# An encoder layer with a mixture of experts: the order of merge, output projection and top-k for two groups of tokens

## Chip, cores, metric

One core of a Trainium2 chip. The metric is the device time of the kernel in microseconds: the median of the runs shown.

## The reference, cut to what matters

One layer is applied to two groups that share all weights: a prompt of 256 tokens (2 tiles of 128) and a sample of 1024 (8 tiles), model width 1024.

```python
h = rms_norm(x) * (1 + sc1) + sh1
[qA|kA|vA|qB|kB|vB|gA|gB] = h @ w_in
oa = global_attention(...) @ w_branch_a          # 8 heads, all keys of the group
ob = window_attention(...) @ w_branch_b          # 8 heads, |i - j| <= 128, "banded"
x  = x + gt1 * ((sigmoid(ga) * oa + sigmoid(gb) * ob) @ w_out)
h2 = rms_norm(x) * (1 + sc2) + sh2
aff = softmax(h2 @ w_router)                     # 16 experts
g, idx = top_k(aff.T, cap)                       # per group; cap 128 (sample), 32 (prompt)
ye = (silu(h2[idx] @ w_gate[e]) * (h2[idx] @ w_up[e])) @ w_down[e] * g
y = rms_norm(x + gt2 * scatter_add(ye, idx))
```

The top-k of a group needs the affinities of all its tokens, and the first expert needs the indices of both groups.

## The kernel before

**Split products.** The projections from the merge on, and the experts, are done as three bf16 products (`split_product`): each operand is cut into a bf16 high half and the rest, low half. So each operand needs a high-half copy and a subtraction first. `HS` does it for the normed input h on POOL, `NM` for attention outputs on POOL, `WS` for a block of merge weights (ScalarE high, VectorE low), `WO` for w_out, POOL inside `M` for the merged activations.

**The plan.** `plan_steps` returns one list of steps. Every engine walks the same list and does its own part of each step, in that order; semaphores tie the parts together. So a step that stands early in the list holds all later ones of the same engine. SyncE has a program of its own that issues the loads in a fixed order, each behind a wait.

**The stages, in order.** Attention items (`S`, `MX`, `EX`, `T`, `PV`); the last 40 items are banded, four to a group, and `HS` of all ten tiles is placed at every second of them. Then the merge: for each m of eight 128-column blocks of the output, `("M", m, c)` computes gA, gB and the two branch projections for 512, 512 and 256 tokens (c = 0, 1, 2; prompt and sample in one row of 1280 tokens). A block's weights (1.5 MB: six DMAs in `mw_load`, rows of 512 bytes) land in one staging area `mw` and are split into one of two buffers `mws`; the next load waits for that split (`ws_done`). Then the projection: `("O", t)` for ten tiles, prompt first; `XO` adds the residual and normalizes, `X2` transposes and modulates, `RT` is router and softmax, `AT` transposes affinities into `affP` or `affS`. `GT` 0 to 3 broadcast gate 1, `GT` 4 to 7 gate 2. `("K", 0)`, the prompt's top-k, stands after the seventh tile; after the last tile come `GT` 4 to 7, `("K", 1)`, the sample's top-k, and `I`, which transposes indices and weights. In `topk` (L1059) a round takes the largest 8 with three scans of the list (L1062 to L1064): 16 rounds over 1024 affinities for the sample, 4 over 256 for the prompt, 16 experts on 16 partitions.

**Experts.** Weights come in chunks of 2 MB: `load_chunk`, three staging areas (`stage`: gate, up, down), split by halves into six slots (ScalarE L803 high, VectorE L1302 low). The first eight halves (`AHEAD`) are prepared before expert 0: ScalarE's high halves in step `("K", 1)`, the low halves by POOL (L751). SyncE sends chunks 0 and 1 of expert 0 after the last output tile (L595) and each further one when a staging area is free. Expert 0's rows are gathered by two indirect DMAs on POOL (L700), transposed, modulated by VectorE (L1294) and split by POOL (L713, L716). Expert 0 has sixteen groups of gate and up products, four to a quarter; later experts also carry the down products of the one before.

## Time and profile before

| | us |
|---|---|
| median of 3 runs | 2573.92 |
| lowest, highest | 2571.49, 2574.54 |
| the profiled execution, its time | 2572.49 |
| its span, first to last instruction | 2570.7 |
| TensorE busy in it | 2384.8 (93%) |
| VectorE busy | 1605.4 (62%) |
| ScalarE busy | 1162.8 (45%) |
| POOL busy | 1123.0 (44%) |
| mean granted TensorE clock | 0.964 of full speed |

The page cuts the span into 40 slices of 64 us and gives the busy share of each engine in tenths. TensorE is at 8 or 9 everywhere but in slices 18 and 19 (1093 to 1221 us) and the last. Busy shares don't say what a stage waits for; the waits, the chain of work that ended last and the timelines do. Engines are named PE (TensorE), DVE (VectorE), ACT (ScalarE), POOL and SP (SyncE) in the rows; `arena` is the one large SBUF buffer that holds nearly all tiles.

### The profile page before, as it was taken

What the parts mean: (1) busy time and instruction counts of PE and PEld (TensorE: products, weight loads), DVE (VectorE), ACT (ScalarE), POOL (GpSimd) and SP (SyncE); (2) the same over time, 40 slices, a digit from 0 to 9 for tenths busy, and PEclk for the clock granted to TensorE, in tenths of its full rate; (3) what the DMA queues carried; (4) which work ended last, traced back from release to release, by engine and by line L of the source; (5) the groups of instructions that cost most, each with busy time, mean ns of one, the idle gap of its engine ahead of it and who ended that gap; (6) DMA issues with size and microseconds to landing.
All of it is one profiled execution on the core that took longest, in us unless ns stands there. A gap on an engine that the chain in (4) does not pass through costs nothing.

```text
span 2570.7 us, 53875 instructions
## 1 busy us (share of the span) xinstructions
PE 2384.8 (93%) x23508; PEld 1712.8 (67%) x23508; DVE 1605.4 (62%) x2014; ACT 1162.8 (45%) x1468; POOL 1123.0 (44%) x721
## 2 busy tenths in 40 slices
PE   8999899998999999934899999999999999999993
PEld 3444477655555555523788888888888888888871
DVE  1643466556111125575888878887888878887862
ACT  2111455567111112330656655665556655556552
POOL 0000111146232331042657667776677666676640
PEclk9999899999999999956999999999999999999997
DMA  8100300220221103252889998999899998999965
GB/s 315 33 17 1 115 1 1 99 99 2 82 50 50 25 34 115 99 207 76 300 317 330 324 318 321 326 336 320 312 331 318 343 315 317 331 330 326 315 234 188
DMA packets 230113, 512.23 MB, mean 199 GB/s; under 512 B 7819, under 2 KB 35580, under 8 KB 229756
## 3 DMA queue, kind: packets, MB, share of 16 engines
q1 hardware_dynamic: 219324, 477.36, 52.3%
q0 software_dynamic: 10560, 31.46, 4.4%
q8 instruction: 186, 3.05, 0.5%
q14 instruction: 43, 0.35, 0.0%
HBM read 480.49 MB, written 28.31 MB: 198 GB/s over the span
## 4 chain that ended last, share of the span: by engine, by line
PE 85%; DVE 6%; POOL 2%; SPq 2%; ACT 1%; DMA 1%; issue 1%; DVEq 0%; POOLq 0%; ACTq 0%
PE ps L1403 21%; PE ps L1404 20%; PE ps L1405 20%; PE ps L1472 7%; PE ps L1688 4%; PE ps L1533 3%; PE ps L1545 3%; PE ps L1514 2%; DVE arena L1054 1%; DVE ti_s L1063 1%; DVE top_s L1062 1%; DVE arena L1064 1%; POOL arena L679 1%; PE ps L1625 1%; POOL arena L676 1%
## 5 line engine op out<-in xcount | busy, mean ns | idle before, releaser
L1403 PE MATMUL ps<-arena 128*128 128x160 bf16 (+2 forms) x5344 | 1308.6, 264 | 21.8 <-DVE arena L1335 8.3
L1404 PE MATMUL ps<-arena 128*128 128x160 bf16 (+2 forms) x5344 | 1308.6, 264 | 0.0
L1405 PE MATMUL ps<-arena 128*128 128x160 bf16 (+2 forms) x5344 | 1308.4, 264 | 0.0
L1302 DVE TENSOR_TENSOR arena<-arena 128x2048 bf16<-128x2048 f32 x376 | 919.2, 2450 | 193.3 <-ACT arena L803 192.3
L803 ACT ACTIVATE arena<-arena 128x2048 bf16<-128x2048 f32 x384 | 726.7, 1904 | 239.0 <-PE ps L1405 176.9
L1403 PEld LDWEIGHTS ps<-arena 128*128 128x128 bf16 x5344 | 524.1, 98 | 154.6 <-issue 27.0
L1405 PEld LDWEIGHTS ps<-arena 128*128 128x128 bf16 x5344 | 524.3, 98 | 127.8 <-issue 1.9
L1404 PEld LDWEIGHTS ps<-arena 128*128 128x128 bf16 x5344 | 524.3, 98 | 118.9 <-issue 1.4
L727 POOL TENSOR_TENSOR arena<-arena 128x320 bf16<-128x320 f32 x128 | 283.8, 2217 | 10.0
L724 POOL TENSOR_TENSOR arena<-arena,ones 128x320 bf16<-128x320 f32 x128 | 179.4, 1401 | 179.3 <-DVE arena L1335 179.0
L991 ACT ACTIVATE arena<-ps 128x160 f32<-128x160 f32 x256 | 77.4, 303 | 351.4 <-PE ps L1405 351.4
L1472 PE MATMUL ps<-arena 128*128 128x512 f32 x480 | 208.1, 593 | 3.0 <-DMA arena<-w_in 1.7
L656 POOL TENSOR_TENSOR arena<-ones,rinv 128x512 f32<-128x512 f32 x20 | 20.9, 1043 | 393.9 <-DVE rinv L1206 337.0
L1240 DVE TENSOR_TENSOR arena<-arena,ps 128x512 f32<-128x512 f32 (+1 forms) x48 | 26.6, 595 | 246.5 <-ACT arena L956 246.5
L1472 PEld LDWEIGHTS ps<-arena 128*128 128x128 f32 x480 | 90.3, 190 | 113.8 <-issue 109.5
L956 ACT ACTIVATE arena<-ps 128x512 f32<-128x512 f32 (+1 forms) x48 | 22.6, 523 | 263.5 <-PE ps L1405 263.5
L686 POOL TENSOR_TENSOR arena<-arena 128x512 f32<-128x512 f32 (+1 forms) x24 | 26.1, 1088 | 217.9 <-DVE arena L1240 217.9
L713 POOL TENSOR_TENSOR arena<-arena,ones 128x480 bf16<-128x480 f32 (+1 forms) x48 | 101.4, 2113 | 45.4 <-DVE arena L1294 45.4
L911 ACT ACTIVATE arena<-ps 128x512 f32<-128x512 f32 (+2 forms) x160 | 74.5, 494 | 102.4 <-PE ps L1533 97.8
L1533 PEld LDWEIGHTS ps<-ident,arena 128*128 128x128 f32 x752 | 81.7, 143 | 55.0 <-issue 44.7
L1054 DVE TENSOR_SCALAR arena<-ps,A,modT 128x128 f32<-128x128 f32 x160 | 52.8, 402 | 97.9 <-PE ps L1458 97.9
L1335 DVE TENSOR_TENSOR arena<-arena,ps 128x160 f32<-128x160 f32 x256 | 79.2, 310 | 55.3 <-POOL arena L727 38.4
(197 smaller groups left out, 2377.8 us busy)
## 6 DMA issues: line engine op xcount, KB each, us to landing
arena<-w_e_gate SPq DMA_DIRECT2D x64, 2048.0 KB, 9.1
arena<-w_e_up SPq DMA_DIRECT2D x64, 2048.0 KB, 9.5
arena<-w_e_down SPq DMA_DIRECT2D x64, 2048.0 KB, 9.2
arena<-w_ada SPq DMA_DIRECT2D x12, 2048.0 KB, 8.6
arena<-x_sample SPq DMA_DIRECT2D x16, 512.0 KB, 3.5
arena<-w_in SPq DMA_DIRECT2D x16, 512.0 KB, 5.3
arena<-w_in SPq DMA_DIRECT2D x3, 2048.0 KB, 21.0
arena<-w_out SPq DMA_DIRECT2D x2, 2048.0 KB, 8.0
```

Source lines behind the costliest of these rows:

```text
L713: gp.tensor_tensor(xeT[par][:, 0, d0:d1], src, ones[:, 0:d1 - d0].unsqueeze(2).to_broadcast([P, d1 - d0, SLOTS]), ALU.mult).then_inc(high, 1)
L724: gp.tensor_tensor(hidT[par][:, 0, f:f + 2], src, ones[:, 0:2].unsqueeze(2).to_broadcast([P, 2, SLOTS]), ALU.mult).then_inc(high, 1)
L727: gp.tensor_tensor(hidT[par][:, 1, f:f + 2], src, hidT[par][:, 0, f:f + 2], ALU.subtract).then_inc(hid_done, 1)
L803: ac.activation(split_half(slot, a)[0], stage_half(kind, a), ACT.Copy).then_inc(hi_done, 1)
L1302: ve.tensor_tensor(lo, stage_half(kind, a), hi, ALU.subtract).then_inc(lo_done, 1)
L1335: ve.tensor_tensor(hid32[:, f % 4], sil[:, f % 2], ps[:, f % 3, SLOTS:2 * SLOTS], ALU.mult)\
L1403: pe.matmul(out, w_hi, x_hi, start=start, stop=False)
L1404: pe.matmul(out, w_hi, x_lo, start=False, stop=False)
L1405: return pe.matmul(out, w_lo, x_hi, start=False, stop=stop)
L1472: ins = pe.matmul(ps[:, n % 5], hT[:, kk, t * P:(t + 1) * P], wqkv[c][:, kk, :], start=(kk == 0), stop=(kk == KD - 1))
L1533: ins = pe.transpose(b[:, q * P:(q + 1) * P], probs(i, hh)[:, (a + q) * P:(a + q + 1) * P], ident[:])
L1688: ins = pe.matmul(ps[32 * g:32 * g + 32, 5, 0:256], x, wv[n][:, kf, 256 * g:256 * g + 256], start=q + kf == 0 and x is x_hi and n == 0, st ...
```

## The change

- The merge runs for the sample alone first: `("M", m, 0)` and `("M", m, 1)`, 512 tokens each. The splits of w_out (`WO`) stand before the last of these parts instead of after it.
- Then the output projection of the eight sample tiles (`O` 0 to 7). Tiles are now numbered by position p, and `tile_at(p)` puts the prompt's tiles last (positions 8 and 9).
- Then the merge for the prompt, `("M2", m, b)`: b = 0, 1 are its two halves, 256 tokens, the same products as the old c = 2. Its eight weight blocks are loaded a second time into the same `mw`, and split into `mws2`: the high half by ScalarE, of the low half 1024 elements by VectorE (`ws_done`) and 2048 by POOL (`ws_rest`). The first two loads and splits are placed among the output tiles; load 2 stands behind all residual loads in SyncE's order, and each next one behind both parts of the split before it. Loads of expert chunks 0 and 1 follow loads 3 and 4.
- The sample's top-k is cut into two half lists of 512 on partitions 0 to 15 and 32 to 47, 16 rounds (`KR`) for both at once, placed between the blocks of `M2` (0, 0, 2, 3, 3, 3, 3, 2 rounds). `KM` merges the two sorted halves in ten small operations. `GT` 4 to 7 are placed inside blocks 3 and 4.
- Then `O` 8 and 9; the last inner step of `O` 8 waits for block 7's merged part. After them the prompt's top-k and `I`.
- `HS` stands at every third banded item, for the sample's eight tiles; the prompt's two come after the attention. q and o are laid out tile by tile.
- The low halves of the first eight expert weight halves are done by VectorE: four before expert 0's rows are modulated and four after.

```diff
+def tile_at(p):
+    return (p + PT_TILES) % NT
...
             c += 1
-        if i >= first_b + 11 and i % 2 and hs < NT:
+        if i >= first_b + 11 and (i - first_b) % 3 == 2 and hs < NT - PT_TILES:
             s.append(("HS", hs))
             hs += 1
         if i == len(items):
             s += [("A2",), ("WS", 0)]
-    assert hs == NT
+    assert hs == NT - PT_TILES
+    s += [("HS", p) for p in range(hs, NT)]
     assert t == len(items) and pv == len(items) and len(normed) == len(items) // NPAIR and s_ac == 12
     for m in range(KD):
         s.append(("M", m, 0))
         if m + 1 < KD:
             s.append(("WS", m + 1))
-        s.append(("M", m, 1))
         if m == KD - 1:
             s += [("WO", 0), ("WO", 1)]
-        s.append(("M", m, 2))
-    for t in range(NT + 3):
-        if t < NT:
-            s.append(("O", t))
-        if t == 0:
+        s.append(("M", m, 1))
+    ns = NT - PT_TILES
+    for p in range(ns):
+        s.append(("O", p))
+        if p == 0:
             s += [("GT", n) for n in range(4)]
-        if 0 <= t - 1 < NT:
-            s.append(("X2", t - 1))
-        if 0 <= t - 2 < NT:
-            s.append(("RT", t - 2))
-        if 0 <= t - 3 < NT:
-            s.append(("AT", t - 3))
-        if t == 6:
-            s.append(("K", 0))
-        if t < NT:
-            s.append(("XO", t))
-    s += [("GT", n) for n in range(4, 8)]
-    s += [("K", 1), ("I",)]
+        if p >= 1:
+            s.append(("X2", p - 1))
+        if p >= 2:
+            s.append(("RT", p - 2))
+        if p >= 3:
+            s.append(("AT", p - 3))
+        s.append(("XO", p))
+        if p in (1, 3):
+            s.append(("WS", KD + p // 2))
+    tail = {(0, 1): [("X2", ns - 1), ("RT", ns - 2), ("AT", ns - 3)], (1, 0): [("RT", ns - 1), ("AT", ns - 2)],
+            (1, 1): [("AT", ns - 1)], (3, 0): [("GT", 4)], (3, 1): [("GT", 5)], (4, 0): [("GT", 6)], (4, 1): [("GT", 7)]}
+    r = 0
+    for m in range(KD):
+        for b in range(2):
+            s.append(("M2", m, b))
+            s += tail.get((m, b), [])
+        if m + 2 < KD:
+            s.append(("WS", KD + m + 2))
+        for _ in range((0, 0, 2, 3, 3, 3, 3, 2)[m]):
+            s.append(("KR", r))
+            r += 1
+    assert r == CAP_S // 8
+    s += [("O", ns), ("KM",), ("XO", ns), ("O", ns + 1), ("X2", ns), ("XO", ns + 1), ("RT", ns), ("AT", ns), ("X2", ns + 1),
+          ("RT", ns + 1), ("AT", ns + 1), ("K", 0), ("K", 1), ("I",)]
     return s
...
-        qT = at(10240, 2, NPAIR, TOK)
+        qT = at(10240, NT, 2 * NPAIR, P)
...
+        hTs = [half_words(RH, 2 * KD, SEQ), half_words(RH + 2048, 2 * KD, DEC)]
+        mergedS = [half_words(8192, 2 * KD, SEQ), half_words(0, 2 * KD, DEC)]
         MW = 3 * KD * P
         mw = 26112
         mws = [20480, 43520]
+        mws2 = [34304, 43520]
         wo = [at(39424, KD, 512), at(24576, KD, 512)]
         sig = at(47616, 2, 2, 512)
-        gt1b = at(33280, 2, D)
+        gt1b = at(31232, 2, D)
         wos = [half_words(20480, 2, CH), half_words(39424, 2, CH)]
+        late = at(33792, 3, CAP_S)
...
+        affS = at(33280, DEC // 2)[0:64]
...
-            def mw_load(m):
+            def mw_load(k):
+                m = k % KD
...
-            sp.wait_ge(mm_ready, 3 * KD)
+            sp.wait_ge(mm_ready, 2 * KD)
...
-                sp.dma_start(xo[:, t], token_rows(x_d, t)).then_inc(xo_in[t], 16)
-            for t in range(NT):
-                if t + 2 < NT:
-                    sp.wait_ge(x1_ready, t + 1)
-                    sp.dma_start(xo[:, t % 2], token_rows(x_d, t + 2)).then_inc(xo_in[t % 2], 16)
+            for p in range(2):
+                sp.dma_start(xo[:, p], token_rows(x_d, tile_at(p))).then_inc(xo_in[p], 16)
+            sp.wait_ge(wos_ready, 4)
+            mw_load(KD)
+            for p in range(NT - 2):
+                sp.wait_ge(x1_ready, p + 1)
+                sp.dma_start(xo[:, p % 2], token_rows(x_d, tile_at(p + 2))).then_inc(xo_in[p % 2], 16)
+                if p == 1:
+                    sp.wait_ge(ws_done, KD + 1)
+                    sp.wait_ge(ws_rest, 1)
+                    mw_load(KD + 1)
+            for k in range(2, KD):
+                sp.wait_ge(ws_done, KD + k)
+                sp.wait_ge(ws_rest, k)
+                mw_load(KD + k)
+                if k in (3, 4):
+                    sp.wait_ge(out_done, NT - PT_TILES)
+                    load_chunk(-1, k - 3)
             sp.wait_ge(out_done, NT)
-            load_chunk(-1, 0)
-            load_chunk(-1, 1)
             load_chunk(0, 2)
...
+                if k == "WS" and s[1] >= KD:
+                    m = s[1]
+                    gp.wait_ge(ws_hi, m + 1)
+                    w = half_words(mws2[m % 2], 2, MW)[:, :, 0:2 * KD * P]
+                    gp.tensor_tensor(w[:, 1], at(mw, 2 * KD * P), w[:, 0], ALU.subtract).then_inc(ws_rest, 1)
...
-            for h in range(AHEAD):
-                gp.wait_ge(hi_done, h + 1)
-                kind, slot = ring(first_half(h))
-                hi, lo = split_half(slot, h % 2)
-                gp.tensor_tensor(lo, stage_half(kind, h % 2), hi, ALU.subtract).then_inc(lo_done, 1)
...
+                    if m in (KD, KD + 1):
+                        ac.wait_ge(m_done, 2 * KD)
+                    elif m > KD:
+                        ac.wait_ge(m2_done, 2 * (m - KD) - 2)
                     ac.wait_ge(mw_in[m % 2], 96 * (m // 2 + 1))
-                    ac.activation(half_words(mws[m % 2], 2, MW)[:, 0], at(mw, MW), ACT.Copy).then_inc(ws_hi, 1)
+                    ac.activation(half_words((mws if m < KD else mws2)[m % 2], 2, MW)[:, 0], at(mw, MW), ACT.Copy)\
+                        .then_inc(ws_hi, 1)
                 if k == "WO":
...
-                        ac.wait_ge(m_done, 3 * KD - 3)
+                        ac.wait_ge(m_done, 2 * KD - 2)
...
+                if k == "M2":
+                    n, b = merge_part(s)[0], s[2]
+                    ac.wait_ge(m2_done, 2 * s[1] + b + 1)
+                    ac.wait_ge(merged_ready, n - 1)
+                    ac.activation(sig[:, n % 2, b, 0:SEQ], ps[:, 2 * (n % 2) + b, 0:SEQ], ACT.Sigmoid).then_inc(sig_ready, 1)
...
+            def top_round(b, r, a):
+                rows = (NE, 64)[b]
+                v = top[b][0:rows, r * 8:r * 8 + 8]
+                link(ve.max(v, a))
+                ve.max_index(ti[b][0:rows, r * 8:r * 8 + 8], v, a)
+                link(ve.match_replace(a, v, a, -1.0))
+            def merge_halves():
+                def backward(x):
+                    x = x[32:32 + NE]
+                    return bass.AP(tensor=x.tensor, offset=x.offset + CAP_S - 1, ap=[x.ap[0], [-1, CAP_S]])
+                link(ve.tensor_copy(tif[1][:], ti[1][:]))
+                v, f = late[0:NE, 0], late[0:NE, 1]
+                ve.tensor_copy(v, backward(top[1]))
+                link(ve.tensor_scalar(f, backward(tif[1]), float(DEC // 2), None, ALU.add))
+                first, pos = top[1][0:NE], tif[1][0:NE]
+                pick = late[0:NE, 2]
+                ve.tensor_tensor(pick, first, v, ALU.is_ge)
+                link(ve.tensor_tensor(pos, pos, f, ALU.subtract))
+                link(ve.tensor_tensor(pos, pos, pick, ALU.mult))
+                ve.tensor_tensor(first, first, v, ALU.max)
+                link(ve.tensor_tensor(pos, pos, f, ALU.add))
+            def topk_prompt():
+                for r in range(CAP_P // 8):
+                    top_round(0, r, affP[:])
+                link(ve.tensor_copy(tif[0][:], ti[0][:]))
+                ve.tensor_copy(top4, top[0][:].unsqueeze(1).to_broadcast([NE, 4, CAP_P]))
+                for g in range(4):
+                    ins = ve.tensor_scalar(tif4[:, g], tif[0][:], 4.0, float(g), ALU.mult, ALU.add)
+                link(ins)
                 ve.engine_nop().then_inc(topk_ready, 1)
...
-                    w = half_words(mws[m % 2], 2, MW)
-                    ve.tensor_tensor(w[:, 1], at(mw, MW), w[:, 0], ALU.subtract).then_inc(ws_done, 1)
+                    a = 0 if m < KD else 2 * KD * P
+                    w = half_words((mws if m < KD else mws2)[m % 2], 2, MW)[:, :, a:]
+                    ve.tensor_tensor(w[:, 1], at(mw, MW)[:, a:], w[:, 0], ALU.subtract).then_inc(ws_done, 1)
...
+                if k == "M2":
+                    n, b = merge_part(s)[0], s[2]
+                    ve.wait_ge(sig_ready, 2 * n + b + 1)
+                    x = sig[:, n % 2, b, 0:SEQ]
+                    ins = ve.tensor_tensor(x, x, ps[:, 2 * (n % 2) + b, SEQ:2 * SEQ], ALU.mult)
+                    if b:
+                        ins.then_inc(mm_ready, 1)
...
+                if k == "KR":
+                    top_round(1, s[1], affS)
+                if k == "KM":
+                    merge_halves()
+                if k == "K" and s[1] == 0:
+                    topk_prompt()
...
+            for h in range(4):
+                split_low(*ring(first_half(h)), h % 2, h + 1)
             for n in range(3):
                 modulate_rows(0, n, 0, first=True)
+            for h in range(4, AHEAD):
+                split_low(*ring(first_half(h)), h % 2, h + 1)
             ve.memset(rst[:, 0, 0:1], 0.0).then_inc(ye_done, 1)
...
+                if k == "M2":
+                    m, b = s[1], s[2]
+                    n = 2 * KD + m
+                    if b == 0:
+                        pe.wait_ge(ws_done, KD + m + 1)
+                        pe.wait_ge(ws_rest, m + 1)
+                        if m == 0:
+                            pe.wait_ge(hs_done, NT)
+                        if m < 2:
+                            pe.wait_ge(out_free, NT - PT_TILES - 1 + m)
+                        else:
+                            pe.wait_ge(mm_ready, n - 1)
...
```

## Rows read from the trace of the kernel before

**Rows 1.** The waits over the span: who waited for whom: us, times, longest.
```profile
PE ps L1638 <- DVEq L1071: 58.3, 1, 58.3
```

**Rows 2.** The waits of TensorE from 1270 us to the end.
```profile
PE ps L1403 <- issue: 4.7, 1, 4.7
```

**Rows 3.** Timeline around the merge: start us, us, engine, line, operation, [idle before].
```profile
645.92 0.39 PE L1403 MATMUL ps<-arena 128*128 128x512 bf16 x1
...
677.21 1.08 ACT L956 ACTIVATE arena<-ps 128x512 f32<-128x512 f32 x2 [11.80 <-PE ps L1405]
...
685.07 0.66 ACT L956 ACTIVATE arena<-ps 128x256 f32<-128x256 f32 x2 [6.78 <-PE ps L1405]
```

**Rows 4.** Windows: stretch, length, busy us of each engine, granted clock, DMA.
```profile
957.40:965.40 8.00, 5.63 (x27) 2.36 (x26) 5.96 (x4) 4.25 (x4) 2.35 (x1) 1.00 0.00 1
...
1065.00:1070.00 5.00, 4.86 (x26) 4.71 (x27) 2.89 (x10) 0.40 (x2) 1.05 (x2) 0.58 0.54 208
```

**Rows 5.** The chain that ended last: start us, us, what.
```profile
1035.27 0.87 PE ps L1458 x8
...
1036.15 1.69 PE ps L1625 x16
...
1048.32 0.45 PE ps L1458 x4
...
1094.74 0.45 PE ps L1458 x4
...
1198.96 0.31 PE ps L1403
```

**Rows 6.** Timeline of VectorE, 1040 to 1183 us.
```profile
1040.91 1.22 DVE L1254 TENSOR_TENSOR arena<-arena 128x1024 f32<-128x1024 f32 x1
...
1052.60 0.41 DVE L1062 MAX8 top_p<-yeP 16x8 f32<-16x256 f32 x1
...
1058.91 1.23 DVE L1252 TENSOR_TENSOR arena<-ps,arena 128x1024 f32<-128x1024 f32 x1
...
1116.41 0.28 DVE L1274 COPY arena<-ps 16x128 f32<-16x128 f32 x1 [0.29 <-PE ps L1631]
...
1122.33 1.21 DVE L1062 MAX8 top_s<-arena 16x8 f32<-16x1024 f32 x1
...
1182.95 0.29 DVE L1283 CAST idx_p<-ps 32x16 uint32<-32x16 f32 x2 [0.35 <-PE ps L1638]
```

**Rows 7.** Timeline of VectorE, the banded attention at 610 us.
```profile
610.05 0.69 DVE L1211 TENSOR_TENSOR arena<-ps,arena 128x512 f32<-128x512 f32 x1 [1.85 <-ACT arena L886]
...
621.54 0.69 DVE L1211 TENSOR_TENSOR arena<-ps,arena 128x512 f32<-128x512 f32 x1 [1.85 <-ACT arena L886]
```

**Rows 8.** Timeline of one weight block of the merge, and POOL at 1127 us.
```profile
668.83 0.37 SPq L534 DMA_DIRECT2D arena<-w_in  x1
...
671.19 2.56 SPq L536 DMA_DIRECT2D arena<-w_branch_b  x2
...
662.64 2.77 ACT L919 ACTIVATE arena<-arena 128x3072 bf16<-128x3072 f32 x1
...
665.44 3.36 DVE L1216 TENSOR_TENSOR arena<-arena 128x3072 bf16<-128x3072 f32 x1 [1.37 <-ACT arena L919]
...
1126.97 16.14 POOL L751 TENSOR_TENSOR arena<-arena 128x2048 bf16<-128x2048 f32 x4 [20.32 <-ACT arena L803]
```

**Rows 9.** Lines L536, L688, L700: landing in us, or count and ns, min/median/max.
```profile
DMA to landing us min/median/max: 4.0/5.1/8.5
...
L688 POOL TENSOR_TENSOR arena<-arena,ones x24: 612/1040/4197, 665.5 to 966.8; 128x512 bf16<-128x512 f32 x16, 128x256 bf16<-128x256 f32 x8
...
L700 POOL DMA_INDIRECT arena<-xn_prompt,gidx_p x16: 880/1310/2876, 1186.1 to 2359.7; - x16
```

**Rows 10.** Timeline of VectorE in expert 0.
```profile
1222.83 2.29 DVE L1302 TENSOR_TENSOR arena<-arena 128x2048 bf16<-128x2048 f32 x1 [0.80 <-ACT arena L803]
```

**Rows 11.** The page, section 6: DMA issues, count, KB each, us to landing.
```profile
arena<-w_e_gate SPq DMA_DIRECT2D x64, 2048.0 KB, 9.1
```

168 lines of the change are left out of this document (87 added, 81 removed).

## Prediction

> **What bounds the kernel now.** I read the table of waits first, over the whole span and then over the expert loop alone. The longest single wait of TensorE is 58.3 us: its index transposes (L1638) wait for VectorE's top-k [rows 1]. From 1270 us to the end TensorE waits once, 4.7 us for issue [rows 2]: the fifteen later experts are TensorE work end to end. So the change can move the end only by moving the start of expert 0's products (1198.96 in the trace, [rows 5]) or by leaving expert 1 a worse queue. I therefore walk one chain: merge start, merge end, end of the sample's output projection (T0), end of the last output tile (X), indices, first expert product.
>
> **Before, stage by stage.** The merge begins at 645.92; its two 512-column parts take (677.21 - 645.92 - 0.3)/2 = 15.5 us each, its 256-column part 685.07 - 677.21 = 7.86 [rows 3]. Eight rounds end at 645.9 + 8 x 38.9 = 957.4. An output tile comes every 13.05 us (1048.32 - 1035.27), but the three from 1048.32 to 1094.74 take 46.4 instead of 39.2 [rows 5]: the prompt's top-k holds VectorE from 1052.60 to 1058.91 [rows 6] and TensorE then restarts at a granted clock of 0.58 [rows 4]. That is 7.3 us. From 1094.74 to the end of the last affinity copy (1116.7) are 22 us, then gate work to 1122.33, the sample's top-k to 1182.95 (60.6), index copies to 1183.8 by my reading, and 15.2 us of gather and row work to 1198.96 [rows 5, 6].
>
> **Merge and projection, after.** Sixteen 512-column parts are 248.6 us. The prompt's eight parts (62.9 us) are not removed but moved behind the sample's projection, so this alone gains nothing. Fewer h splits per item free POOL, but a group of four banded items still takes 621.54 - 610.05 = 11.49 us once the splits have ended [rows 7], and four splits with the group's three other POOL steps fill just that, so I give it 1 us (bounds 0 and 2.5). The prompt's two h splits (8 us) run while POOL is idle in the first merge part. Merge end: 645.9 - 1 + 248.6 = 893.5. The w_out splits now start one 512-column part ahead of the end, which removes the idle 8.0 - 5.6 = 2.4 us at 957.4 [rows 4]. Eight output tiles then end at T0 = 893.5 + (1048.32 + 13.05 - 957.4) - 2.4 = 995. The two weight splits put between tiles find 2 to 3 us of room in the 13.05 and cost nothing; without that room 1 us each. The changed layouts of q and o keep the same instructions: nothing.
>
> **The prompt's merge, where I expect the gain to go.** TensorE has 62.9 us of products here, and the sixteen half-list rounds lie beside them. A round is three scans; a scan of 256 takes 0.41 us and one of 1024 1.21 [rows 6], so one of 512 takes 0.68, a round 2.15 and sixteen 34 us, against 60.6. But the weights of each block are loaded a second time into the one staging area `mw`, and load k+1 may start only when block k is split (ws_done and ws_rest). Before, a period was 38.9 us and hid that. Now one turn is: the load, from 668.83, whose last two issues at 671.19 take 2.56 us and which lands a median 5.1 us (at most 8.5) after issue, so 8.4 (bounds 7.4 and 9.5) [rows 8, 9]; ScalarE's high half 2.8; POOL's 2048-element subtraction 16.14/4 = 4.0 [rows 8]; and VectorE's 1024-element subtraction, 1.1, a third of 3.36, which I add because POOL's copy of 1.04 us (median) took up to 4.20, and that one began as VectorE's 3.36 us subtraction ran [rows 8, 9]. With 0.3 for semaphores that is 16.6 us a turn, against 7.9 of products. The first loads are done under the projection; load 2 stands in SyncE's queue behind x1_ready(8), 7 us after T0 (a residual sum that starts at 1040.91 for a tile whose products end just before the 1035.27 of [rows 5]; [rows 6]), lands at 15.8, and waits there some 1.5 us behind the softmax and sigmoid in ScalarE's queue, so block 2 is ready at T0 + 17.3 + 2.8 + 5.2 + 0.2 = T0 + 25.5. TensorE by then has done blocks 0 and 1 and the last router tiles. Five turns more: 5 x 16.6 = 83. To that come the two expert chunks that SyncE sends behind loads 3 and 4 (1.5 us each, bounds 0 and 3), 0.8 for multiplies on the port, and an in-order coupling: gate broadcasts 4 and 6 stand in VectorE's queue behind the next WS and its rounds of top-k (4.3 and 6.5 us), and TensorE waits for each of their diagonals before the second half of blocks 3 and 4. ScalarE's copies of broadcasts 5 and 7 then end at 11.3 and 13.2 us into a turn, ahead of a split whose data is there at 8.4, so these turns are 3.2 and 5.0 longer. Block 7 is ready at T0 + 25.5 + 83 + 3 + 0.8 + 8.2 = T0 + 120.5. After an idle stretch of 8 us its products start at the lower clock (0.58 in [rows 4]): 10.1 us, not 7.9. The last rounds, the list merge of some ten small operations (3 us) and POOL's merge lie under the next tile. Two tiles of 10.3 (13.05 less 0.87 for transposes, 1.69 for the router and 0.2, [rows 5]): X = T0 + 120.5 + 10.1 + 20.6 = T0 + 151.2 = 1146.
>
> **Tail.** From X: X2(8), the residual of tile 9, softmax of 8, then X2, router and softmax of 9 at the lower clock, without two older tiles between: 20.0 us against 22. Then the prompt's top-k, 6.3, moved here from where it cost 7.3, and the copies: indices at X + 27.4 = 1173.6 (before 1183.8). Gate broadcasts are gone from here.
>
> **Expert 0's start.** The first eight weight halves were split by POOL under the top-k; now VectorE does them, 2.29 us each [rows 10], four right after the indices and four amid the row work. The first four hold it 9.2 us, longer than the gather that they stand behind, and in the trace the gather's POOL instruction takes 0.88 us free and up to 2.88 in the expert loop, where such subtractions run beside it [rows 9]. I take 4 us for the gather and 5 for the row splits held by halves 5 to 8 (bounds of the sum 2 and 11): products start 24.2 instead of 15.2 us after the indices, at 1197.8. The chunks after the first two are loaded only from then on (9.1 us to landing, [rows 11]); they land some 5 us before the end of the first quarter of products (13.3 us warm), after which the order is the old one.
>
> The Trainium skill, SBUF — State Buffer, section "Who interferes with whom", says that a VectorE instruction with two SBUF inputs blocks a POOL instruction that reads SBUF but, as an inference, not descriptor generation. The first half agrees with the 4.20 us row. The second does not with the 2.88. By it the gather would leave on time, 4 us earlier, and the sum would be 2567 us; I give it 3 in 10, inside the first rival.
>
> **Sum.** First product at 1197.8 instead of 1199.0: 1.2 us gained against the profiled execution's 2572.5 (span 2570.7, some 2 around it), so 2571.3. The median of the runs shown, 2573.9, lies 1.4 above that execution; I say 2572.
>
> **Rivals.** (1) The loop is bare. If ScalarE's copies don't meet the splits and the chunks don't slow the loads, the 8.2 + 3 us go, with the gather's 4 and a warm block 7 (2.2): 17 us, 2554. For it: each is a coincidence of a few us. Against: the queue orders are in the code. (2) The second loading is hidden altogether and TensorE sets the pace: block 7's products end 73 us after T0, not 130.6: 2514. Against it: 8.4 + 2.8 + 5.2 with one staging area can't be under 7.9. (3) Slower: the lost cover of expert 0. Before, four chunks were split and two more staged when the products began; now two are split. If chunk 7 lands after the first quarter of products, the 5 us of room gone, expert 0 runs at the pace of loading and splitting two staging areas, about 9.1 + 1.9 + 4 x 1.15 = 15.6 us a quarter against 13.3, which over four quarters with the start costs 9 to 12 us: 2582. For it: VectorE now does lows and rows in one queue. (4) The change doesn't hide the top-k: VectorE's 34 us of rounds could miss the waits and stand after X, up to 2600; the plan puts all sixteen before the last two tiles, so this is only the tail of (3).
>
> **Chances.** A measurement tells 0.2%, 5.1 us. Forecast 0.42, mostly within that: 0.10 faster, 0.28 no difference, 0.04 slower. Rival 1 0.28: 0.25 faster, 0.03 no difference. Rival 2 0.05 faster. Rivals 3 and 4 0.25: 0.04 no difference, 0.21 slower. Together 0.40, 0.35, 0.25. The range leaves out rival 2 and the ends of 1 and 3: 2552 to 2586; the forecast's own is 2563 to 2580.
>
> **What would show it.** The wait of the top-k transposes (58.3) is gone. In the prompt's merge TensorE waits 6 to 9 us before each block from the third on, for POOL's new subtraction, blocks are 16 to 22 us apart, SyncE's six-piece loads come once a block, and the granted clock falls to about half in slices there. Indices lie 9 to 12 us earlier, the first expert product 0 to 5 us. If the blocks are 8 us apart, rival 2 holds; if TensorE waits inside expert 0 for more than before, rival 3. I am wrong in the main step if the turn isn't 16 us or more.

## The result, and the profile after

| | before | after |
|---|---|---|
| median, us (8 runs each) | 2573.49 | 2580.18 |
| lowest, highest | 2570.56, 2575.80 | 2577.71, 2582.69 |
| span of the profiled execution | 2570.7 | 2578.6 |
| POOL copies the first row indices | 1183.96 | 1177.90 |
| first product of expert 0 | 1198.96 | 1206.09 |
| from there to the end of the span | 1371.7 | 1372.5 |

After over before is 1.0027 [1.0017, 1.0038]: 6.7 us slower. The prediction was 2572, no difference; the change is slower by more than the 0.2% that a measurement tells. The last three lines of the table hold the whole case. The indices are 6.1 us earlier, the first product 7.1 us later, and what follows it is as long as before.

The page of the kernel after: busy time and count of each engine, the granted clock in tenths by slices of 64 us, and DMA packets by size.

```profile
PE 2381.7 (92%) x23418; PEld 1713.2 (66%) x23508; DVE 1617.4 (63%) x2038; ACT 1187.4 (46%) x1478; POOL 1147.4 (44%) x721
...
PEclk9999999999999999786999999999999999999997
...
DMA packets 255458, 524.82 MB, mean 204 GB/s; under 512 B 8587, under 2 KB 60924, under 8 KB 255100
```

TensorE's busy time is what it was (2384.8 before). The low clock lies in slices 17 to 19. The waits of TensorE in the kernel after, 990 to 1290 us: who waited for what, us in total, times, longest.

```profile
PE ps L1644 <- DVE arena L1298: 26.4, 4, 12.4
PE ps L1484 <- issue: 16.0, 3, 9.6
PE ps L1759 <- DMA arena<-xn_prompt,gidx_p: 15.6, 1, 15.6
PE ps L1745 <- DVE af L1338: 9.7, 3, 4.7
PE ps L1484 <- POOL arena L760: 8.8, 1, 8.8
PE ps L1484 <- DVE arena L1416: 7.8, 1, 7.8
PE ps L1752 <- DVEq L1137: 6.6, 1, 6.6
```

The 58.3 us of [rows 1] are gone (6.6 are left, the prompt's list). In their place stand 26.4 us for the gate broadcasts, which the kernel before didn't wait for, waits inside the prompt's merge that the profile files under issue, 15.6 us for the gathered rows instead of 6.4, and 8.8 us for POOL's row splits instead of 4.9.

**The prompt's merge.** Four timelines of the kernel after: start us, us, engine, line, operation, [idle before <- releaser]. First SyncE's first piece of each load from load 3 on, then ScalarE's high half of blocks 2 to 7, then POOL's low half of blocks 2 and 7, then three of the four groups of matmuls that make TensorE's gate broadcasts.

```profile
1023.97 0.37 SPq L561 DMA_DIRECT2D arena<-w_in  x1
...
1040.64 0.37 SPq L561 DMA_DIRECT2D arena<-w_in  x1
...
1057.03 0.37 SPq L561 DMA_DIRECT2D arena<-w_in  x1
...
1078.97 0.37 SPq L561 DMA_DIRECT2D arena<-w_in  x1
...
1102.67 0.37 SPq L561 DMA_DIRECT2D arena<-w_in  x1
```

```profile
1015.95 2.77 ACT L961 ACTIVATE arena<-arena 128x3072 bf16<-128x3072 f32 x1 [4.78 <-DMA arena<-w_branch_b]
...
1032.63 2.76 ACT L961 ACTIVATE arena<-arena 128x3072 bf16<-128x3072 f32 x1 [8.84 <-DMA arena<-w_branch_b]
...
1049.02 2.76 ACT L961 ACTIVATE arena<-arena 128x3072 bf16<-128x3072 f32 x1 [13.08 <-DMA arena<-w_branch_b]
...
1070.95 2.77 ACT L961 ACTIVATE arena<-arena 128x3072 bf16<-128x3072 f32 x1
...
1094.66 2.76 ACT L961 ACTIVATE arena<-arena 128x3072 bf16<-128x3072 f32 x1
...
1112.30 2.76 ACT L961 ACTIVATE arena<-arena 128x3072 bf16<-128x3072 f32 x1 [9.89 <-DMA arena<-w_branch_b]
```

```profile
1018.79 5.10 POOL L735 TENSOR_TENSOR arena<-arena 128x2048 bf16<-128x2048 f32 x1 [8.41 <-ACT arena L961]
...
1115.14 5.10 POOL L735 TENSOR_TENSOR arena<-arena 128x2048 bf16<-128x2048 f32 x1 [7.07 <-ACT arena L961]
```

```profile
1058.62 2.04 PE L1644 MATMUL ps<-arena,ones 128*128 128x128 f32 x8 [12.43 <-DVE arena L1298]
...
1069.00 1.13 PE L1644 MATMUL ps<-arena,ones 128*128 128x128 f32 x8 [2.65 <-DVE arena L1298]
...
1082.72 2.04 PE L1644 MATMUL ps<-arena,ones 128*128 128x128 f32 x8 [8.67 <-DVE arena L1298]
```

The chain of one turn can be read across them. Load 4 is issued at 1040.64 and lands at 1049.02 (8.4 us), ScalarE takes 2.8, POOL 5.1, and load 5 goes out at 1057.03: 16.4 us. The next high half doesn't run at about 1065.4, when by the same 8.4 us its data is in, but at 1070.95: on ScalarE it stands behind the copy of a broadcast whose matmul ran at 1069.00. So that turn is 21.9 us and the one after it 23.7. The last turn, from 1094.66 to 1112.30, has no broadcast and takes 17.6.

**Expert 0's start.** The timeline of VectorE, POOL and SyncE in the kernel after, from the copies of the indices on.

```profile
1177.64 8.89 DVE L1381 TENSOR_TENSOR arena<-arena 128x2048 bf16<-128x2048 f32 x4
1177.90 2.06 POOL L796 COPY gidx_p<-idx_p 32x1 uint32<-32x1 uint32 x1 [16.84 <-DVE gv_s L1362]
1179.91 2.25 POOL L796 COPY gidx_s<-idx_s 128x1 uint32<-128x1 uint32 x1
1182.15 0.37 SPq L604 DMA_DIRECT2D arena<-w_e_gate  x1
1182.44 2.80 POOL L744 DMA_INDIRECT arena<-xn_sample,gidx_s  x1 [0.28 <-POOL gidx_s L796]
1185.55 1.74 POOL L744 DMA_INDIRECT arena<-xn_prompt,gidx_p  x1 [0.30 <-issue]
1186.55 0.37 SPq L604 DMA_DIRECT2D arena<-w_e_up  x1
...
1200.46 2.77 POOL L757 TENSOR_TENSOR arena<-arena,ones 128x320 bf16<-128x320 f32 x1
...
1203.31 2.72 POOL L760 TENSOR_TENSOR arena<-arena 128x320 bf16<-128x320 f32 x1
```

And the gather's piece of the chain that ended last (start us, us, what), first of the kernel before, then of the kernel after.

```profile
1186.11 3.73 DMA arena<-xn_prompt,gidx_p
```

```profile
1185.55 7.45 DMA arena<-xn_prompt,gidx_p
```

From the index copy to the second gather's issue are 7.65 us (before: 1186.11 - 1183.96 = 2.15), the landing takes 3.7 us more, and from there to the first product are 13.1 us instead of 9.1. The three differences are 5.5 + 3.7 + 4.0 = 13.2.

### The profile page after: what moved, and what is told of

It reads as the page before. It is cut to its first block, busy times and chain, and to the rows that moved or that the text cites. A ratio compares the mean times of both kernels' runs of the same rounds, so it can differ in the third digit from the quotient of the medians.

```text
span 2578.6 us, 53904 instructions
## 1 busy us (share of the span) xinstructions
PE 2381.7 (92%) x23418; PEld 1713.2 (66%) x23508; DVE 1617.4 (63%) x2038; ACT 1187.4 (46%) x1478; POOL 1147.4 (44%) x721
## 4 chain that ended last, share of the span: by engine, by line
PE 84%; DVE 5%; DMA 3%; SPq 2%; ACT 2%; issue 2%; POOL 2%; DVEq 0%; ACTq 0%; POOLq 0%
PE ps L1485 20%; PE ps L1486 20%; PE ps L1484 19%; PE ps L1553 7%; PE ps L1802 4%; PE ps L1626 3%; PE ps L1614 3%; PE ps L1595 2%; DVE arena L1100 1%; DMA arena<-w_branch_b 1%; PE ps L1605 1%; ACT arena L961 1%; POOL arena L735 1%; PE ps L1635 1%; PE ps L1759 1%
## 5 line engine op out<-in xcount | busy, mean ns | idle before, releaser
L1381 DVE TENSOR_TENSOR arena<-arena 128x2048 bf16<-128x2048 f32 x384 | 940.3, 2454 | 190.0 <-ACT arena L841 189.5
L771 POOL TENSOR_TENSOR arena<-arena 128x320 bf16<-128x320 f32 x128 | 275.9, 2155 | 10.0
L768 POOL TENSOR_TENSOR arena<-arena,ones 128x320 bf16<-128x320 f32 x128 | 185.8, 1451 | 176.9 <-DVE arena L1416 176.7
L1305 DVE TENSOR_TENSOR arena<-arena,ps 128x512 f32<-128x512 f32 x32 | 20.6, 685 | 185.2 <-ACT arena L998 185.2
L1614 PE MATMUL ps<-ident,arena 128*128 128x128 f32 x752 | 109.8, 284 | 3.1 <-ACT arena L938 1.4
L998 ACT ACTIVATE arena<-ps 128x512 f32<-128x512 f32 x32 | 17.4, 595 | 202.9 <-PE ps L1486 202.9
```

Of the source, the lines that this page charges most:

```text
L768: gp.tensor_tensor(hidT[par][:, 0, f:f + 2], src, ones[:, 0:2].unsqueeze(2).to_broadcast([P, 2, SLOTS]), ALU.mult).then_inc(high, 1)
L771: gp.tensor_tensor(hidT[par][:, 1, f:f + 2], src, hidT[par][:, 0, f:f + 2], ALU.subtract).then_inc(hid_done, 1)
L1381: ve.tensor_tensor(lo, stage_half(kind, a), hi, ALU.subtract).then_inc(lo_done, 1)
L1614: ins = pe.transpose(b[:, q * P:(q + 1) * P], probs(i, hh)[:, (a + q) * P:(a + q + 1) * P], ident[:])
```

## The experiments

Line numbers in the variants shift by the lines put in. "First product" is that of expert 0. The last column is the profiled span less the first product: but for two rows it stays within 1371.3 and 1372.7. The two columns before it come from a single profile, and one execution lies up to 3 us from its kernel's median: in e5 and e6, which change nothing ahead of the indices, these stand 3.5 and 2.2 us earlier than in the kernel after. So sizes are better taken from the medians, or from times counted from the indices on. Some expectations use names that don't fit the kernel: the "attention's" items, loads and transposes behind the merge are those of the output tiles and of the affinities, and the "low halves of h" in e6 are those of the expert's weights.

| kernel | median, us | over before, 95% | indices | first product | rest |
|---|---|---|---|---|---|
| before | 2573.5 | 1 | 1183.96 | 1198.96 | 1371.7 |
| after | 2580.2 | 1.0027 [1.0017, 1.0038] | 1177.90 | 1206.09 | 1372.5 |
| e8 before, half lists alone | 2556.8 | 0.9935 [0.9920, 0.9951] | 1164.68 | 1180.98 | 1372.7 |
| e7 before, h at every third | 2575.6 | 1.0008 [0.9999, 1.0017] | 1184.27 | 1199.18 | 1372.0 |
| e1 after, broadcasts in block 1 | 2569.4 | 0.9984 [0.9975, 0.9993] | 1167.20 | 1195.28 | 1371.7 |
| e2 after, two landing areas | 2547.7 | 0.9902 [0.9887, 0.9917] | 1144.64 | 1172.90 | 1372.0 |
| e3 after, split on VectorE | 2576.5 | 1.0014 [1.0005, 1.0023] | 1172.43 | 1200.41 | 1371.8 |
| e4 after, load 2 early | 2576.9 | 1.0014 [1.0005, 1.0023] | 1173.62 | 1202.10 | 1372.7 |
| e5 after, chunks behind the gather | 2573.2 | 1.0003 [0.9994, 1.0012] | 1174.39 | 1194.97 | 1373.2 |
| e6 after, low halves behind rows | 2583.5 | 1.0040 [1.0026, 1.0054] | 1175.67 | 1198.99 | 1380.9 |
| e9 = e1 + e2 | 2531.2 | 0.9833 [0.9817, 0.9848] | 1128.99 | 1157.62 | 1372.5 |
| e10 after, slots turned | 2567.5 | 0.9978 [0.9969, 0.9987] | 1177.15 | 1192.18 | 1371.4 |
| e11 = e1 + e2 + e10 | 2519.6 | 0.9790 [0.9775, 0.9805] | 1129.87 | 1144.77 | 1371.8 |
| e12 e11, broadcasts by tile | 2567.0 | 0.9976 [0.9966, 0.9986] | 1178.05 | 1193.05 | 1371.9 |
| e13 after, all broadcasts first | 2572.7 | 0.9992 [0.9983, 1.0001] | 1170.83 | 1199.19 | 1372.1 |
| e14 after, chunks late | 2580.2 | 1.0025 [1.0016, 1.0034] | 1177.55 | 1205.95 | 1372.0 |
| e15 = e2 + e10 + e13 + e14 | 2513.7 | 0.9768 [0.9753, 0.9783] | 1125.36 | 1140.38 | 1371.3 |

**e8, the half lists without the new order.** The kernel before, its order untouched; the list moves to 64 partitions, then `KM`'s ten operations.

```diff
-                        dst = affS[:, (t - PT_TILES) * P:(t - PT_TILES + 1) * P]
+                        u = t - PT_TILES
+                        if u == 0:
+                            link(ve.memset(affS, -1.0))
+                        dst = affS[32 * (u // 4):32 * (u // 4) + NE, u % 4 * P:(u % 4 + 1) * P]
...
                 link(ve.tensor_copy(tif[b][:], ti[b][:]))
+                if b == 1:
+                    merge_halves()
```

> The kernel before, with its order of matmuls untouched and the sample's top-k alone as two half lists; the whole computation is there. Theory (the half lists are a gain wherever they stand, since the 32 rounds of 1.81 us are on the path to the first expert product in the kernel before): the list goes from 60.6 us to 34.6 + 2.4 for the joining, so the indices come at about 1160 instead of 1183.8, and the whole is some 20 to 24 us shorter, 2550 to 2554. Rival (other work holds the gather anyway, the ten low halves on POOL that end near 1161, or the copies of the last sample items): under 8 us, 2566 or more.

TensorE's wait for the list in this run, beside [rows 1], and its wait for the rows:

```profile
PE ps L1661 <- DVEq L1091: 38.4, 1, 38.4
...
PE ps L1668 <- DMA arena<-xn_prompt,gidx_p: 7.7, 1, 7.7
```

19.9 us less of the one, 1.3 more of the other, 0.9935: the theory's mechanism, 3 us short of its size. (The expectation counts 32 rounds of 1.81 us; the list of the kernel before has 16 of 3.8.) So one part of the change alone gains 17 us, and the new order with all that hangs on it, as it was built, costs 23 (2580.2 - 2556.8).

**e7, the thinner splits of h.** The kernel before with `(i - first_b) % 3 == 2`.

> The kernel before, with POOL's split of a tile of h at every third banded item instead of every second; nothing is left out. Theory (POOL has room in that stage and its end is set by the list, not by the splits): the time stays within 2 us of 2573.5. Rival (the ten splits end later than the list and hold the start of expert 0): 5 to 15 us slower.

No difference by its interval, as expected. It is not where the time went.

**e2, two landing areas.** Blocks 1, 3, 5 and 7 land elsewhere, so that the next load is behind the split of the block before the last one. The edit also moves loads: load 1 no longer waits for the split of block 0, and load 2 is sent among the output tiles, at 950.05 instead of 1003.41, which is the change of e4 below.

```diff
                 if p == 1:
+                    mw_load(KD + 1)
+                if p == 3:
                     sp.wait_ge(ws_done, KD + 1)
                     sp.wait_ge(ws_rest, 1)
-                    mw_load(KD + 1)
-            for k in range(2, KD):
-                sp.wait_ge(ws_done, KD + k)
-                sp.wait_ge(ws_rest, k)
+                    mw_load(KD + 2)
+            for k in range(3, KD):
+                sp.wait_ge(ws_done, KD + k - 1)
+                sp.wait_ge(ws_rest, k - 1)
```

> The changed kernel, with a second landing area for the prompt's merge weights, so that load k+1 is issued while block k's weights are still being split; nothing is left out. Theory (from load 2 on each turn is load 8.4 us, ScalarE half 3.4, POOL low half 5.1 in series, and TensorE waits for it at each block): the turn falls from 16.6 us at the shortest to about 9 to 11, blocks 2 to 7 end some 40 us earlier, and the kernel takes 2535 to 2545. Rival (the waits in those blocks are the copies of the attention's and gate's tiles and the matmuls themselves, which would be late anyway): under 15 us, 2565 to 2578.

POOL's low halves of blocks 2 to 7 in this run:

```profile
1012.17 5.11 POOL L742 TENSOR_TENSOR arena<-arena 128x2048 bf16<-128x2048 f32 x1 [3.52 <-ACT arena L970]
...
1020.78 5.12 POOL L742 TENSOR_TENSOR arena<-arena 128x2048 bf16<-128x2048 f32 x1
...
1028.93 5.09 POOL L742 TENSOR_TENSOR arena<-arena 128x2048 bf16<-128x2048 f32 x1 [0.29 <-ACT arena L970]
...
1050.56 5.10 POOL L742 TENSOR_TENSOR arena<-arena 128x2048 bf16<-128x2048 f32 x1 [4.37 <-ACT arena L974]
...
1074.00 5.11 POOL L742 TENSOR_TENSOR arena<-arena 128x2048 bf16<-128x2048 f32 x1 [3.98 <-ACT arena L970]
...
1085.45 4.06 POOL L742 TENSOR_TENSOR arena<-arena 128x2048 bf16<-128x2048 f32 x1
```

32.5 us, on the theory's side and 3 us short of its range. Two turns fall to 8.6 and 8.2 us, then come 21.6 and 23.4, and the last is 11.5. The serial turn of load and split was the main cost: of the 32.5 us some 3 to 4 belong to the earlier load 2 (e4), the other 29, by difference, to the landing areas. What is left are the two turns with broadcasts, as long as before: they don't hang on the loads at all.

**e1, the broadcasts earlier.**

```diff
-            (1, 1): [("AT", ns - 1)], (3, 0): [("GT", 4)], (3, 1): [("GT", 5)], (4, 0): [("GT", 6)], (4, 1): [("GT", 7)]}
+            (1, 1): [("AT", ns - 1)] + [("GT", n) for n in range(4, 8)]}
```

> The changed kernel, with the four gate broadcasts GT 4 to 7 moved out of blocks 3 and 4 to the place right behind the last transposes of the attention; nothing is left out. Theory (blocks 5 and 6 took 21.9 and 23.7 us where blocks 3 and 4 took 16.7 and 16.4, and the broadcasts that wait for VectorE's rows, 26.4 us of waits on the matmuls of this line, are what lengthens them): blocks 5 and 6 fall to about 17, 10 to 12 us less in all, 2568 to 2570. Rival (the wait is only moved to block 2, where the same rows are later still, or the splits set the pace and the broadcasts lie in their shadow): within 3 us of 2580.

(The broadcasts stand in block 1, counted from 0; where an expectation says block 2, it is the second block.) TensorE's wait for the diagonals, 990 to 1290 us:

```profile
PE ps L1644 <- DVE arena L1298: 2.5, 2, 2.4
```

The wait for the diagonals falls from 26.4 to 2.5 us and the first product comes 10.8 us earlier. The theory holds.

**e9, e1 and e2 together.**

> The changed kernel with both the second landing area and the early gate broadcasts; nothing is left out. Theory (in the run with the second landing area alone, blocks 3, 4 and 5 of the prompt's merge still took 17.6, 23.8 and 15.5 us, where 6 and 7 took 7.4 and 7.9, and the broadcasts stand in them): these three fall to 8 to 10 us each, so 25 to 33 us go on top of the 32.5 that the area brought, 2515 to 2523. Rival (with both gone VectorE's rounds of the half lists, 16 of 2.16 us and up to three in a block, hold the evacuations, or the load of 8.4 us and more sets the pace): blocks of 11 to 14 us, 2530 to 2540.

16.5 us on top of e2: the rival's side. POOL's subtractions then start at 1014.42, 1031.71, 1039.27, 1049.97, 1061.42 and 1069.78. The first turn is long because ScalarE's high half stands behind the four copies; later ones are 7.6 to 11.5 us, and VectorE (three rounds of 2.16, 1.2 and 0.8) and POOL (5.1 and 2 to 3) each have some 8 us of work in a block.

**e4, load 2 earlier.** It is issued at 965.29 instead of 1003.41.

```diff
+                if p == 4:
+                    sp.wait_ge(ws_done, KD + 2)
+                    sp.wait_ge(ws_rest, 2)
+                    mw_load(KD + 2)
-            for k in range(2, KD):
+            for k in range(3, KD):
```

> The changed kernel, with the merge's second prompt load issued after the attention's fourth item instead of after its last, so that it no longer stands behind the last attention load on the queue; nothing is left out. Theory (block 2 was late by T0 + 28.0 us because this load took 12.5 us from its issue at 1003.4): blocks 2 to 7 all come 4 to 8 us earlier, 2572 to 2576. Rival (the landing area is free only at that moment, because it waits for the split of block 1, so the issue does not move): within 1.5 us of 2580.2.

POOL's first low half starts at 1014.05 instead of 1018.79, the first product comes 4.0 us and the end 3.3 us earlier: between the two, nearer to the theory. The rival's reason (the area isn't free) is false: load 2 does go out 38 us earlier.

**e3, the whole split on VectorE.** POOL's part and its semaphore are taken out, `a = 0` for every block.

> The changed kernel, with VectorE alone making the low halves of the merge weights for blocks 2 and later, and POOL none; nothing is left out. Theory (the turn is load 8.4, high half 3.4, then POOL's 5.10 us; VectorE does the same 3072 columns in about 2.8 at 0.9 ns a column, so each turn is up to 2.3 us shorter): 6 turns give 8 to 14 us if VectorE has the time, 2566 to 2572. Rival (VectorE's own queue, with the attention's copies, the gate's rows and the list, holds each split, or the list ends later): within 4 us of 2580.2, or slower.

3.7 us: the rival. The expectation's 2.8 us at 0.9 ns a column stands in no run: the 3072-column subtraction takes VectorE 3.36 us here and in the kernel after, so a turn could gain 1.7 us and not 2.3. POOL's last merge steps of blocks 2 to 7 follow each other after 27.0, 26.3, 16.7, 14.5 and 7.1 us, where in the kernel after they do after 26.8, 24.0, 14.6, 17.6 and 8.3, and block 2 comes 2.0 us sooner: turns with a free VectorE are shorter, those in which it has broadcasts and three rounds are longer.

**e14, the chunk loads later**, `if k in (6, 7)` for `(3, 4)`.

> The changed kernel with the two chunk loads of the first expert behind loads 6 and 7 of the merge weights instead of behind 3 and 4; nothing is left out. Theory of the record (each delays the next merge load by 1.5 us): 3 us less, 2577. Rival (a 2 MB load has landed before the next merge load is issued, 16 us later, and costs nothing): within 1.5 us of 2580.2.

Nothing at all (2580.24). The loads go out at 1024.23, 1041.08 and 1057.38, as with the chunks between them. The rival holds.

**e5, the chunk loads behind the gather.**

```diff
                 sp.wait_ge(lo_done, 2 * n + 2)
+                if n == 0:
+                    sp.wait_ge(gat[0], 16)
+                    sp.wait_ge(gat[1], 16)
                 load_chunk(-1, c)
```

> The changed kernel, with SP waiting for both halves of the gather's rows before it issues the first expert's chunk loads that come after the third; nothing is left out. Theory (two 2 MB-class loads issued at 1182.15 and 1186.55 share the 16 DMA engines with the gather, whose second half took 7.45 us instead of 3.73 before): the second half lands in about 3.8 us, the first product comes 3 to 4 us earlier, 2576 to 2577, if expert 0 still finds its chunks. Rival A (the gather is as slow by itself, its rows are only issued later): within 1 us of 2580.2. Rival B (expert 0 runs at the pace of its loads, which now start 6 to 10 us later): the gather is faster and the time is the same or up to 6 us more.

The gather's piece of the chain in this run, and POOL's last row split:

```profile
1182.03 3.82 DMA arena<-xn_prompt,gidx_p
```

```profile
1193.33 0.72 POOL L760 TENSOR_TENSOR arena<-arena,ones 128x320 bf16<-128x320 f32 x1
1194.13 0.79 POOL L763 TENSOR_TENSOR arena<-arena 128x320 bf16<-128x320 f32 x1
```

The landing falls from 7.45 to 3.82 us, which shows that the chunk loads had slowed it. The gain is 7.0 us, twice what I expected. The other half is at the rows: the chunk now lands later, so VectorE's next subtractions, which wait for its high half, start behind POOL's last row split (1195.78) and no longer beside it, and that split takes 0.72 and 0.79 us instead of 2.77 and 2.72. From the indices to the first product it is 7.6 us less, 3.6 by the landing and 4.0 by the row split. The same gather lands in 7.2 to 7.9 us in all eight runs that keep the after kernel's order of these loads, and in 3.6 to 3.8 in the eight in which no chunk load is issued in the 10 us before it or before it has landed.

**e6, the low halves behind the rows.** The first loop of four is joined to the second.

> The changed kernel, with POOL's and VectorE's first four low halves of h behind the modulation of the first rows instead of ahead of them; nothing is left out. Theory (the first product waits for the gathered rows, 15.6 us on TensorE, and the low halves stand in front of the gather's preparation: POOL's two copies of 2.06 and 2.25 us, and descriptor work of 2.80 and 1.74 beside VectorE's 8.89 us operations): rows come 3 to 5 us earlier, but the wait for the low half of h that stood behind them (8.8 us) grows by about as much or more: within 3 us of 2580.2, with the two waits exchanged. Rival (the gather's issue is what counts and the low halves have slack): 3 to 6 us shorter.

POOL's index copies and gather, then the first product of expert 0 with TensorE's wait before it, then that wait's line in the table of waits from 1190 us on:

```profile
1175.67 0.18 POOL L796 COPY gidx_p<-idx_p 32x1 uint32<-32x1 uint32 x1 [16.84 <-DVE gv_s L1362]
1175.79 0.17 POOL L796 COPY gidx_s<-idx_s 128x1 uint32<-128x1 uint32 x1
1176.46 1.04 POOL L744 DMA_INDIRECT arena<-xn_sample,gidx_s  x1 [0.49 <-POOL gidx_s L796]
1177.81 0.89 POOL L744 DMA_INDIRECT arena<-xn_prompt,gidx_p  x1 [0.30 <-issue]
```

```profile
1198.99 0.29 PE L1482 MATMUL ps<-arena 128*128 128x160 bf16 x1 [13.27 <-DVE arena L1381]
```

```profile
PE ps L1482 <- DVE arena L1381: 15.6, 3, 13.3
```

With VectorE idle the same four POOL instructions take 0.18, 0.17, 1.04 and 0.89 us. But the first product now waits 13.3 us for the low halves, so from the indices to it are 23.3 us, only 4.9 less than in the kernel after. Inside expert 0, whose next halves are late too, 8.4 us are lost (1380.9 in the last column, the only run in which it is longer). The waits are exchanged, as the theory says, at a loss of 3.4 us.

**e10, the start as it was before.** The six split slots are turned by three, so that the first chunks' halves don't lie on the buffers of the last output tiles; the first four low halves go back to POOL.

```diff
-        split = [(3 + n) * CH for n in range(6)]
+        split = [(3 + (n + 3) % 6) * CH for n in range(6)]
...
+                if k == "KM":
+                    for h in range(2):
+                        split_first(h)
...
+                if k == "KM" or k == "RT" and s[1] == NT - PT_TILES:
+                    for h in (0, 1) if k == "KM" else (2, 3):
+                        kind, slot = ring(first_half(h))
+                        gp.wait_ge(hi_done, h + 1)
+                        hi, lo = split_half(slot, h % 2)
+                        gp.tensor_tensor(lo, stage_half(kind, h % 2), hi, ALU.subtract).then_inc(lo_done, 1)
...
-            for h in range(4):
-                split_low(*ring(first_half(h)), h % 2, h + 1)
             for n in range(3):
                 modulate_rows(0, n, 0, first=True)
+            ve.wait_ge(xe_ready, 3)
```

> The changed kernel with the first expert's weight slots turned by three, so that the first chunk's halves can be split right behind block 7 and the second's behind the last output tile, the four low halves on POOL and VectorE's next ones only behind the first rows; nothing is left out. Theory (28.4 us from the indices to the first product against 15.2 in the kernel before are POOL's copies and descriptors at 2 to 3 us beside VectorE's splits, the chunk loads that share the DMA engines with the gather, and the last two row splits at 2.77 and 2.72): all four go and the first product comes 11 to 14 us earlier, 2567 to 2570. Rival (the four low halves on POOL from about 1160 on stand in front of the index copies, or the high halves delay the last tile's gate on ScalarE): under 5 us, 2575 or more.

From indices to product 15.0 us (28.2 in the kernel after), 12.7 us in the time: the theory holds in place and size. The edit changes several things at once; e5 and e6 are the runs that take them one by one.

**e11, e1 + e2 + e10.**

> The changed kernel with the second landing area, the early gate broadcasts and the turned slots together; nothing is left out. Theory (the three lie one behind the other on the path to the first product, so they add): some 11 to 14 us under the run with the first two, 2502 to 2512. Rival (with the blocks that fast the first expert's chunks, loaded at blocks 3 and 4, or the 16 rounds of the list hold the start): 2520 or more.

11.6 us under e9, so e10's gain adds; the total was missed because e9's was.

**e12, one broadcast to each of the output tiles 2 to 5**, with e14's edit, on e11.

> The three repairs together, with the gate broadcasts moved further up, one to each of the sample's output tiles 2 to 5, and the first expert's two chunk loads moved from behind loads 3 and 4 of the merge weights to behind loads 6 and 7; nothing is left out. Theory (in the run with the three repairs block 3 waits some 5 us for ScalarE's high half, which stands behind its copies of the four broadcasts at 1024 to 1029, and load 4 took 10.3 us and came late, with a 2 MB chunk load in front of it): block 3 comes 5 us and block 5 3 to 4 us earlier, 2510 to 2514. Rival (VectorE and POOL each have about 8.3 us of work in a block and set the pace from block 4 on, so that only the first of the two counts, or the broadcasts now lengthen the output tiles): 2515 to 2519.

TensorE's wait for the diagonals, 880 to 1290 us:

```profile
PE ps L1671 <- DVE arena L1326: 42.5, 5, 16.3
```

47 us worse than e11, neither theory nor rival. In each of the four tiles TensorE, which otherwise runs ahead of VectorE, now waits for a diagonal that stands in VectorE's queue behind the tile before (8.5, 16.3, 8.8 and 8.8 us). From 960 to 973 it does nothing at all, and its granted clock in that stretch is 0.55. It is the coupling of e1 once more, at its full size.

**e13, all eight broadcasts behind the first output tile**, on the kernel after. The wait for the diagonal buffer (`n % 4 >= 2`) becomes `n >= 2`, and ScalarE waits for the last merged part.

> The changed kernel with all eight gate broadcasts in one row behind the first output tile's products, none in the prompt's merge; nothing is left out. Theory (in the prompt's merge each broadcast ties TensorE to VectorE's queue and ScalarE's copies to the splits, behind the first tile VectorE and ScalarE have nothing else in front of them): some 14 to 16 us less than the changed kernel, that is the 10.8 of the run with the broadcasts in block 2 and the 4 us that block 3 there still waited, 2564 to 2567. Rival (behind the first tile the four more broadcasts hold the second tile's products and the loads set the pace in the merge): 8 to 11 us less, 2569 to 2572.

7.5 us, a little under the rival. POOL's last merge step of block 0 starts at 1014.78 instead of 1009.71, that of block 7 at 1126.26 instead of 1133.34: 12.1 us less in the prompt's merge. Ahead of it are 5.1 more, 0.7 of them there before the projection starts and the rest in it, where four more broadcasts hold the tiles. So the broadcasts' place in blocks 3 and 4 costs 12 us, and no place that was tried is free.

**e15, e2 + e10 + e13 + e14.**

> The second landing area, the turned slots, all eight broadcasts behind the first output tile and the two chunk loads behind loads 6 and 7; nothing is left out. Theory (the run with one broadcast in each output tile lost 50 us in the tiles, but its blocks 2 to 7 took 55.7 us where they took 63.2 in the run with the three repairs): 6 to 9 us under 2519.6, 2510 to 2514. Rival (the broadcasts cost in the output projection wherever they stand there): 2519 or more.

2513.7 us, 0.9768 of before [0.9753, 0.9783]: faster than both kernels by over 2%, and in the theory's range. It doesn't tell e14's edit from e13's here.

## Right and wrong, step by step

| step of the prediction | reckoned | measured |
|---|---|---|
| end of the sample's projection, T0 | 995 | 995.8 |
| block 2 ready | T0 + 25.5 | 1023.9 = T0 + 28.1 |
| a turn without broadcasts | 16.6 | 16.7, 16.4, and 17.6 for the last |
| broadcasts in two turns | + 8.2 | 21.9 + 23.7 - 2 x 16.55 = + 12.5 |
| two chunk loads | + 3 | 0 (e14) |
| block 7 ready | 1115.5 | 1120.2 |
| last output tile, X | 1146 | 1151.4 |
| X to indices | 27.4 | 26.3 |
| indices to first product | 24.2 | 28.4 |
| first product | 1197.8 | 1206.1 |
| expert 0 and the rest | as before | 0.8 longer than before |

**Right.** The start of expert 0's products is what moves the end. The 58.3 us wait goes, and one landing area makes turns of 16.4 to 17.6 us (e2 shows it: two areas give 8.6 and 8.2, and take some 29 us off). Rival 2 (hidden loading) was far off. Of rival 1, the bare loop, only the free chunk loads came true. The merge and the projection of the sample are within 1 us. Rival 3 gave the nearest time, 2582, by a mechanism that didn't happen: expert 0 isn't longer, its chunks come in time.

**Wrong: the size of two terms.** The steps that failed are the term of the gate broadcasts, reckoned at 8.2 us and 12.5 in the rows, and the one of expert 0's start, reckoned at 9.0 us over the kernel before and 13.2 in the rows. Their signs and places were right; the sum was 8.3 us short because each was some 4 us too small. The other errors cancel, and that is luck: the chunk loads (3), the multiplies (0.8) and the tail (1.1) came out lower, load 2 (2.6), the last turn (1.1), T0 (0.8) and the last tiles (0.5) higher.

*The broadcasts.* The prediction followed VectorE's queue to the first diagonal of each block, and from there it had ScalarE's copies end 11.3 and 13.2 us into the turn. They end 13.9 and 15.7 us into it (1070.93 after load 5 went out at 1057.03, 1094.66 after load 6 at 1078.97). In that stretch lie the first broadcast's matmuls (2.04 us), the second half of the block's products (5.7 us, where a half takes 62.9/16 = 3.9 in the kernel before: the granted clock from 1058.6 to 1066.4 is 0.65), a second wait for a diagonal (2.65) and the second broadcast's matmuls (1.13). The prediction gives a time for none of them, so how the missing 2.5 us a turn divides among them stays open. The whole cost of the place is shown: taking the broadcasts out gives 10.8 us (e1) and 12.1 in the prompt's merge (e13).

*Expert 0's start.* The 4 us for a gather behind VectorE's subtractions were a little low for POOL's instructions (5.5), the 5 for the rows a little high (4.0). What was missing altogether is the third part, 3.7 us: SyncE sends chunk 3 as soon as two low halves are done, 0.3 us before POOL's first gather instruction, and chunk 4 while the second gather is under way. I had written that these loads start "only from then on" and had asked only whether they come in time, not what they collide with. e5 shows it, and e10 removes all three parts.

**Wrong: smaller things.** Load 2 took 12.5 us from its issue to landing (1003.41 to 1015.95), where I took 8.4 and 1.5 for ScalarE's queue; e4 prices its lateness at 3.3 to 4. Why it alone takes 12.5 isn't settled: its last two pieces take 3.43 us to issue where the others' take 1.60, and while it is under way POOL sends the last sample tile's two stores (1006.93 and 1007.46, 1.05 MB together); no run separates the two or shows either to be the cause. The chunk loads cost nothing because they have landed before the next merge load, 16 us later.

**The chances.** They put 0.40 on faster and 0.25 on slower, since rival 1 took whole terms away. But both large errors were pieces left out of a chain of waits, and a piece left out can only make the chain longer: the open ends lay on the slower side. Of the signs that it named, the blocks 16 to 22 us apart and the low clock came (16.4 to 23.7 us, slices 17 to 19); the indices were 6.1 us earlier and not 9 to 12, and the first product was 7.1 us later and not up to 5 earlier. The time is inside the range of 2552 to 2586 and just past the forecast's own upper end of 2580.

## What to carry to other kernels

Before work is moved to fill a wait, ask whether the wait can be made shorter where it is: the half lists alone gained 17 us, and the reordering around them, as it was built, cost 23. It wasn't a bad order, though: with its waits repaired (e15) it is 43 us faster than the half lists alone. When a stage of 39 us a step becomes one of 8, every chain that the old step covered (load, high half, low half through one landing area) becomes the pace, so count its landing areas first. A step that makes TensorE wait for something made in another engine's queue takes away the lead that TensorE has over it; place it where that queue is empty, and price every piece of it: the queue that makes the operand, the step itself at the clock that a wait leaves, and the queue that empties the result.
